# Expert weights on ScalarE, sums of gathered experts in pairs, and selection waits at their use

## The chip, the cores and the metric

The kernel is one program on one core of a Trainium2 chip. The metric is the device time of that core in microseconds. The core's engines are TensorE (PE), VectorE (DVE), ScalarE (ACT), GpSimd (POOL) and SyncE (SP), each with its own stream of instructions in a fixed order, which wait for one another by semaphores, and 16 DMA engines shared by all queues.

## The reference

One layer of a streaming encoder on x of 1024 tokens by 1024 channels, all in float32.

- Mixer: h = adaLN(RMSNorm(x)); an input projection gives q, k, v for stick-breaking attention (8 heads of 64, strictly causal), q, k, v for sliding-window attention (8 query heads, 2 key heads, chunks of 64, two chunks seen, ALiBi and sinks), and two gates. Each branch is projected to 1024 channels, they are merged with sigmoid gates, and x gets gate1 times the output projection.
- Channel part (PEER): h2 = adaLN(RMSNorm(x)). For each token and each of 8 heads: 2 x 128 sub-key scores, top 16 of each half, 256 candidate sums, top 16 of these. That gives 128 experts per token, of 16384. Each expert is one row u and one row v of 1024 floats:

```
act = gelu(h2 . u[e])            exact gelu
w   = softmax(best scores)[e] * act
y   = sum over the token's 128 experts of w * v[e]
x   = x + gate2 * y, then a final RMSNorm
```

## The kernel before

**Gathers.** The table `uv` holds each expert's u and v side by side, 8 KB a row. Tokens are worked in 8 blocks of 128. A block has 128 tiles, and a tile is 128 gathered rows: of 32 tokens, four experts each (partition 32 q + t). GpSimd issues one indirect DMA per tile (L524) into a ring of RING = 10 slots (`ring`), after it has waited for `vs_done` of the group of tiles to which the tile 10 before belongs (L522). The i-th tile serves token group c = i % 4 (32 tokens each).

**What a tile goes through.** VectorE multiplies the u half with the tokens' replicated h2 row (`h2rep[:, c]`) and sums it into one column of `dots` (L1371). For each group of STEP = 4 tiles ScalarE makes gelu of four columns (L1086, `gl`). VectorE multiplies with the gates (L1383, `wv`), and multiplies a stack of four 32x32 unit matrices (`istack`) by these per-partition weights (L1386, `dg`, 128x32 per tile). TensorE multiplies `dg` with the v half, in two halves of 512 columns, into the PSUM banks VACC and VACC+1, one 32-row band per token group (L874); that sum over a block's 128 tiles is y. Its last matmul counts `vs_done`, which frees the ring slots.

**At the end of a block** VectorE takes y out of PSUM (L1397) once all sums of the block are done, and the first sums of the next block wait for that (`fin_y`). Before it, the next block's h2 rows are replicated: for each token group c, four times TensorE (L860) and ScalarE (L1078, `rep_ev`) pass a 256-column piece over one PSUM bank (MISC), each step waiting for the one before; ScalarE's copy for c waits until the old block's last dot product with `h2rep[:, c]` is done.

**Selection** of the experts (`keys`, VectorE) runs in 32 chunks (2 heads of a block each) some 64 tiles ahead: max, max_index, match_replace and so on, each of which waits for the one before through `link` (class Chain: the instruction counts a semaphore and the engine waits for it at once). Between the steps the stream yields, so dot products come in. `gates` makes the softmax's Exp and copies the published indices and gates (L1056, L1062, L1064).

**The mixer** runs in three groups of 2, 3 and 3 blocks (SIZE). The first (g=0) comes before all gathers; the other two run beside the gathers of earlier blocks. Its stages in order: H (norm), V, QK and SB (four head pairs of stick-breaking attention, `pair`), SWP and SW (windowed attention), MG (merge), OUT, PREP (the scores for the selection). Weights are loaded by SP's queue. In SB, ScalarE does Abs, Exp, Ln and again Exp per step (L1017, L1022, L1027, L1035) between TensorE and VectorE.

**The order of the work** is written by `interleave`: every stream yields places, counted in tiles, and the engine's instructions are emitted by rising place. `Plan` gives the mixer's items their places: an item of so many microseconds takes us / rate places, with RATES = (1.9, 3.1, 2.0) for the three groups; g=1 begins at place 0, g=2 at place 235. The tile streams have the places i (dot of tile i), 4(n+1) - 0.9 (gelu of group n), 4(n+1) - 0.4 (weights), 4(n+1) - 0.2 (sums); the replicates for block b have 128 b - 3.6 + c on TensorE and 128 b - 3.5 + c on ScalarE. Since each engine runs its stream in order, an instruction that waits holds back everything of that engine that has a later place.

**ScalarE's function tables** are loaded by an instruction of their own, which `Tables.use` (L98) puts ahead of a function if another table is active at that point of the order: GELU (also used for Tanh), EXP_LN, SQRT. Copy, Abs and Square need no change of table.

Of the kernel before, what the change touches and what calls it, by code (L numbers as in the profile page):

```python
# [14 lines left out]
P = 128  # L15
# [24 lines left out]
RATES = (1.9, 3.1, 2.0)  # L40
# [4 lines left out]
STEP = 4  # L45
# [32 lines left out]
class Chain:  # L78
# [101 lines left out]
def build(nc, x, c8, w_ada, b_ada, g1, g2, gf, w_v, w_qk, w_sw, sinks, w_mg, w_out, w_q, sk, uv, consts,  # L180
          x1_dram, h2_dram, mods_dram, k_dram, v_dram, s_dram, out):
    with ExitStack() as ctx:
# [3 lines left out]
        def sem(name):  # L186
            return ctx.enter_context(nc.semaphore(name))
# [35 lines left out]
        wv = sb("wv", [P, 8])  # L223
# [56 lines left out]
        dve_own = sem("dve_own")  # L280
# [28 lines left out]
        dots_done, gelu_done, dg_done, vs_done = sem("dots_done"), sem("gelu_done"), sem("dg_done"), sem("vs_done")  # L309
# [25 lines left out]
        with nc.Block() as block:  # L335
# [192 lines left out]
            def _(pe):  # L528
# [353 lines left out]
            def _(act):  # L882
# [218 lines left out]
            def _(dve):  # L1101
                link = Chain(dve, dve_own)

# [180 lines left out]
                def keys():  # L1284
                    def top16(values, indices, scores):
                        apart(dve, dve_steps)
                        link(dve.max(values[:, 0:8], scores))
                        yield
                        apart(dve, dve_steps)
                        link(dve.max_index(indices[:, 0:8], values[:, 0:8], scores))  # L1290
                        yield
                        apart(dve, dve_steps)
                        link(dve.match_replace(scores, values[:, 0:8], scores, LOWEST))
                        yield
                        apart(dve, dve_steps)
                        link(dve.max(values[:, 8:16], scores))
# [173 lines left out]
```

## Time and profile before

| | |
|---|---|
| median of 3 runs | 3722.71 us (3718.5 to 3725.89) |
| profiled execution, own time | 3718.71 us |
| its span, first to last instruction | 3716.9 us |
| mean granted TensorE clock | 0.765 |
| busy: PE / DVE / ACT / POOL | 2262.8 / 2161.4 / 685.8 / 1137.3 us |
| moved by DMA | 1276.05 MB, mean 343 GB/s |
| first gather issued, last gather issued | 446.4 and 3689.2 us |

Times in the rows below are microseconds from the start of the span unless they are marked ns. A row of a window gives each engine's busy time with its number of instructions, then the granted TensorE clock, the mean busy share of the 16 DMA engines and the GB/s. A row of a group gives the count, total busy time and mean ns of one, and the idle time of the engine just before them with what ended it. "L874" is line 874 of the kernel. The profiled execution's time is 1.8 us over its span.

### The profile page before, as it was taken

What the parts mean: (1) busy time and instruction counts of PE and PEld (TensorE: products, weight loads), DVE (VectorE), ACT (ScalarE), POOL (GpSimd) and SP (SyncE); (2) the same over time, 40 slices, a digit from 0 to 9 for tenths busy, and PEclk for the clock granted to TensorE, in tenths of its full rate; (3) what the DMA queues carried; (4) which work ended last, traced back from release to release, by engine and by line L of the source; (5) the groups of instructions that cost most, each with busy time, mean ns of one, the idle gap of its engine ahead of it and who ended that gap; (6) DMA issues with size and microseconds to landing.
All of it is one profiled execution on the core that took longest, in us unless ns stands there. A gap on an engine that the chain in (4) does not pass through costs nothing. (4 is left out here: it accounts for less than half of the span.)

```text
span 3716.9 us, 34683 instructions
## 1 busy us (share of the span) xinstructions
PE 2262.8 (61%) x11240; PEld 998.4 (27%) x11240; DVE 2161.4 (58%) x5280; ACT 685.8 (18%) x1587; POOL 1137.3 (31%) x1033
## 2 busy tenths in 40 slices
PE   4678766875987837677776877683433343334333
PEld 2466623333433412232233432341000000000000
DVE  1011444666556465777767766566576767776754
ACT  1210113522102111544422002110100010001000
POOL 0000112322223233333333423334344434443443
PEclk8889868987998967888887989786565556556656
DMA  6414557887799998999988998999899989998998
GB/s 261 171 72 164 194 214 300 340 330 287 315 370 372 362 403 324 352 369 374 355 354 355 422 421 339 374 420 419 351 396 421 417 338 421 421 420 335 421 421 338
DMA packets 196254, 1276.05 MB, mean 343 GB/s; under 512 B 21260, under 2 KB 38700, under 8 KB 54632
## 3 DMA queue, kind: packets, MB, share of 16 engines
q0 software_dynamic: 147616, 1074.03, 71.3%
q1 hardware_dynamic: 48456, 199.80, 13.8%
q8 instruction: 89, 1.46, 0.2%
q14 instruction: 93, 0.76, 0.1%
HBM read 1249.35 MB, written 24.40 MB: 343 GB/s over the span
## 5 line engine op out<-in xcount | busy, mean ns | idle before, releaser
L524 POOL DMA_INDIRECT arena<-in_uv,idx_r x1024 | 1134.2, 1108 | 2552.5 <-PE pb L874 1873.9
L1371 DVE CUSTOM_DVE_ANT_0 arena<-arena 128x1024 f32<-128x1024 f32 x1024 | 1250.9, 1224 | 440.3 <-DMA arena<-in_uv,idx_r 419.6
L874 PE MATMUL pb<-arena,dg 128*32 128x512 f32 x4096 | 757.7, 878 | 946.1 <-DVE dg L1386 939.0
L874 PEld LDWEIGHTS pb<-arena,dg 128*32 128x32 f32 x4096 | 136.0, 140 | 1466.0 <-DVE dg L1386 1159.7
L1086 ACT ACTIVATE gl<-dots 128x4 f32<-128x4 f32 x256 | 52.4, 205 | 1347.0 <-DVE dots L1371 1346.1
L659 PE MATMUL pb<-arena 128*128 128x384 f32 (+1 forms) x768 | 253.4, 488 | 60.2 <-DMA arena<-in_sk 32.9
L98 ACT ACT_TABLE_LOAD x178 | 228.4, 1283 | 241.2 <-DVE dots L1371 196.4
L594 PE MATMUL pb<-arena 128*128 128x384 f32 (+1 forms) x768 | 238.0, 465 | 27.5 <-DMA arena<-in_w_mg 27.5
L1383 DVE TENSOR_TENSOR wv<-gl,gate_r 128x4 f32<-128x4 f32 x256 | 41.2, 161 | 308.8 <-ACT gl L1086 275.9
L659 PEld LDWEIGHTS pb<-arena 128*128 128x128 f32 x768 | 154.3, 206 | 151.1 <-issue 78.0
L594 PEld LDWEIGHTS pb<-arena 128*128 128x128 f32 x768 | 147.8, 195 | 115.9 <-issue 49.5
L860 PE MATMUL pb<-arena,ident 128*32 128x256 f32 x1024 | 109.4, 509 | 71.7 <-ACT arena L1078 62.2
L623 PE MATMUL pb<-arena 128*128 128x512 f32 x256 | 123.2, 635 | 48.4 <-DMA arena<-in_w_out 47.5
L679 PE MATMUL pb<-arena 128*128 128x384 f32 (+1 forms) x384 | 128.0, 492 | 38.4 <-DMA arena<-in_w_qk 38.4
L1255 DVE SCALAR_TENSOR_TENSOR arena<-pb,arena 128x384 f32<-128x384 f32 (+2 forms) x120 | 51.7, 472 | 145.5 <-ACT arena L1027 124.4
L597 PE MATMUL pb<-arena 128*128 128x384 f32 (+1 forms) x384 | 116.8, 455 | 0.0
L679 PEld LDWEIGHTS pb<-arena 128*128 128x128 f32 x384 | 78.0, 208 | 90.7 <-DMA arena<-in_w_qk 41.4
L707 PE MATMUL pb<-arena,tri 128*128 128x384 f32 (+2 forms) x240 | 95.0, 489 | 8.7 <-DVE arena L1255 8.1
L1215 DVE SCALAR_TENSOR_TENSOR arena<-arena,pb 128x384 f32<-128x384 f32 (+1 forms) x48 | 24.4, 508 | 123.0 <-PE pb L597 119.1
L597 PEld LDWEIGHTS pb<-arena 128*128 128x128 f32 x384 | 72.6, 191 | 45.0 <-issue 9.8
L1371 DVE DVE_READ_ACCUMULATOR2_ANT dots<- 128x1 f32 x1024 | 84.1, 82 | 0.0
L721 PE MATMUL pb<-arena 128*64 128x384 f32 (+2 forms) x240 | 62.9, 467 | 31.9 <-ACT arena L1035 28.9
(153 smaller groups left out, 2211.9 us busy)
## 6 DMA issues: line engine op xcount, KB each, us to landing
arena<-in_w_mg SPq DMA_DIRECT2D x24, 1536.0 KB
arena<-in_w_ada SPq DMA_DIRECT2D x12, 2048.0 KB, 17.3
arena<-in_w_q SPq DMA_DIRECT2D x24, 1024.0 KB
arena<-in_uv,idx_r POOLq DMA_INDIRECT x1024
arena<-in_w_qk SPq DMA_DIRECT2D x12, 1024.0 KB, 13.0
arena<-in_w_out SPq DMA_DIRECT2D x3, 4096.0 KB, 16.3
arena<-in_w_sw SPq DMA_DIRECT2D x3, 3072.0 KB, 13.9
arena<-in_x SPq DMA_DIRECT2D x16, 512.0 KB, 20.0
```

What stands on the lines that cost most here:

```text
L98: self.act.add_instruction(mybir.InstLoadActFuncSet(name=self.nc.get_next_instruction_name(), act_func_set_id=table, engine=mybir.EngineTy ...
L524: pool.indirect_dma_start(ring[:, i % RING, :], None, uv, bass.IndirectOffsetOnAxis(ap=idx_r[:, b % 2, 4 * n + c:4 * n + c + 1], axis=0)). ...
L594: m = pe.matmul(bank, wmg[ft % 2][:, q * KT + k, :], hT[:, k, 0:T], start=(k == 0), stop=(k == KT - 1))
L597: m = pe.matmul(bank, wmg[ft % 2][:, 16 + (q - 2) * 4 + k, :], y[:, k, 0:T], start=(k == 0), stop=(k == 3))
L623: m = pe.matmul(pb[:, BGB + 2 * (j % 2) + i, :], merged[:, k, j * P:(j + 1) * P], wout[:, k, i * HALF:(i + 1) * HALF], start=(k == 0), sto ...
L659: m = pe.matmul(pb[:, BGB + p, 0:T], wq[h % 2][:, p, k, :], h2T[:, k, 0:T], start=(k == 0), stop=(k == KT - 1))
L679: m = pe.matmul(pb[:, BGB + i, 0:T], wqk[p % 2][:, i * KT + k, :], hT[:, k, 0:T], start=(k == 0), stop=(k == KT - 1))
L707: m = pe.matmul(pb[:, BGB + c % 4, 0:T - lo], tri[:], spl[:, c % 4, 0:T - lo], start=False, stop=True, skip_group_check=True)
L721: pe.matmul(pb[64 * e:64 * e + 64, AVB, lo:T], vp[:, s, 64 * e:64 * e + 64], zl[:, c % 4, 0:T - lo], start=(i == 0), stop=(s == 0), skip_g ...
L860: x_ = pe.matmul(pb[32 * q:32 * q + 32, MISC, 256:512], selector(c), h2cur[:, 256 * i:256 * i + 256], start=True, stop=True)
L874: m = pe.matmul(pb[32 * c:32 * c + 32, VACC + i, :], dg[:, STEP * n // 4 % 2, c, :], ring[:, (STEP * g + c - first) % RING, D + i * HALF:D ...
L1371: dve.tensor_tensor_reduce(u, h2rep[:, c, :], u, 1.0, 0.0, ALU.mult, ALU.add, dots[:, i % 8:i % 8 + 1]).then_inc(dots_done, 1)
```

## The change

- `STEP` becomes 2: gelu, weights, sums and the release of ring slots go by two tiles. RATES become (1.9, 2.9, 1.9).
- VectorE's stream `weights` and the buffer `wv` go. ScalarE makes `ig` = istack times the gate (one Copy with a per-partition scale for each tile, place 2(g+1) - 2.5), then the gelu (place 2(g+1) + 0.0), and after waiting for both of them and for a free `dg`, `dg` = ig times gelu, again one Copy for each tile.
- TensorE's sums move from place 4(n+1) - 0.2 to 2(n+1) + 0.8.
- The dot products get a wait for the gelu eight tiles back, since nothing else on VectorE now orders the two.
- In `keys`, `link` becomes `step.mark` at the instruction and `step.hold` ahead of the next one, after the yield; with a semaphore of its own (`dve_keys`). `tk_used` is now counted by the last step on the scores.

The diff, cut to its core:

```diff
@@ -37,12 +37,12 @@
 GROUP = [g for g in range(GROUPS) for _ in range(SIZE[g])]
 GMAX = max(SIZE)
 TMAX = GMAX * P
-RATES = (1.9, 3.1, 2.0)
+RATES = (1.9, 2.9, 1.9)
 
 RING = 10
 TILES = 128
 QUADS = TILES // 4
-STEP = 4
+STEP = 2
 STEPS = TILES // STEP
 CHUNKS = 4
 PER_CHUNK = 32
@@ -80,8 +80,14 @@
         self.eng, self.sem, self.n = eng, sem, 0
 
     def __call__(self, ins):
+        self.mark(ins)
+        self.hold()
+
+    def mark(self, ins):
         ins.then_inc(self.sem, 1)
         self.n += 1
+
+    def hold(self):
         self.eng.wait_ge(self.sem, self.n)
 
 
@@ -865,7 +871,7 @@
                         for n in range(STEPS):
                             g = STEPS * b + n
                             first = STEP * n % 4
-                            yield TILES * b + STEP * (n + 1) - 0.2
+                            yield TILES * b + STEP * (n + 1) + 0.8
                             pe.wait_ge(dg_done, g + 1)
                             if n == 0 and b:
                                 pe.wait_ge(fin_y, b)
@@ -1078,12 +1084,27 @@
                                 act.activation(h2rep[:, c, 256 * i:256 * i + 256], pb[:, MISC, 256:512], ACT.Copy).then_inc(rep_ev, 1)
 
                 def gelus():
-                    for g in range(NB * STEPS):
-                        yield STEP * (g + 1) - 0.9
-                        act.wait_ge(dots_done, STEP * (g + 1))
-                        table.use(GELU)
-                        a = STEP * g % 8
-                        act.activation(gl[:, a:a + STEP], dots[:, a:a + STEP], ACT.Gelu).then_inc(gelu_done, 1)
+                    for b in range(NB):
+                        for n in range(STEPS):
+                            g = STEPS * b + n
+                            a, first, half = STEP * g % 8, STEP * n % 4, STEP * n // 4 % 2
+                            yield STEP * (g + 1) - 2.5
+                            if STEP * n % PER_CHUNK == 0:
+                                act.wait_ge(pub_g, CHUNKS * b + STEP * n // PER_CHUNK + 1)
+                            for c in range(STEP):
+                                op = act.activation(ig[:, half, first + c], istack[:], ACT.Copy, scale=gate_r[:, b % 2, STEP * n + c:STEP * n + c + 1])
+                            op.then_inc(ig_done, 1)
+                            yield STEP * (g + 1) + 0.0
+                            act.wait_ge(dots_done, STEP * (g + 1))
+                            table.use(GELU)
+                            act.activation(gl[:, a:a + STEP], dots[:, a:a + STEP], ACT.Gelu).then_inc(gelu_done, 1)
+                            act.wait_ge(gelu_done, g + 1)
+                            act.wait_ge(ig_done, g + 1)
+                            if STEP * g >= 8:
+                                act.wait_ge(vs_done, g + 1 - 8 // STEP)
+                            for c in range(STEP):
+                                op = act.activation(dg[:, half, first + c], ig[:, half, first + c], ACT.Copy, scale=gl[:, a + c:a + c + 1])
+                            op.then_inc(dg_done, 1)
 
                 def final():
                     for b in range(NB):
@@ -1284,17 +1306,21 @@
                 def keys():
                     def top16(values, indices, scores):
                         apart(dve, dve_steps)
-                        link(dve.max(values[:, 0:8], scores))
+                        step.mark(dve.max(values[:, 0:8], scores))
                         yield
+                        step.hold()
                         apart(dve, dve_steps)
-                        link(dve.max_index(indices[:, 0:8], values[:, 0:8], scores))
+                        step.mark(dve.max_index(indices[:, 0:8], values[:, 0:8], scores))
                         yield
+                        step.hold()
                         apart(dve, dve_steps)
...
                                 op = yield from top16(vals[q][:, h, :], kidx[q][:, h, :], tk[:, n % 2, 256 * h + 128 * q:256 * h + 128 * q + 128])
+                                if h + q == 2:
+                                    op.then_inc(tk_used, 1)
+                                else:
+                                    step.mark(op)
                                 yield
-                        op.then_inc(tk_used, 1)
                         dve.wait_ge(tk_used, n + 1)
-                        link(dve.tensor_tensor(cand, vals[0][:].unsqueeze(3).to_broadcast([P, 2, TOPK, TOPK]),
-                                               vals[1][:].unsqueeze(2).to_broadcast([P, 2, TOPK, TOPK]), ALU.add))
+                        step.hold()
+                        step.mark(dve.tensor_tensor(cand, vals[0][:].unsqueeze(3).to_broadcast([P, 2, TOPK, TOPK]),
+                                                    vals[1][:].unsqueeze(2).to_broadcast([P, 2, TOPK, TOPK]), ALU.add))
                         yield
+                        step.hold()
                         for h in range(2):
-                            op = yield from top16(best[:, h, :], bidx[:, h, :], cand[:, h].rearrange("p i j -> p (i j)"))
...
@@ -1367,24 +1405,10 @@
                                 dve.wait_ge(gathered[i % RING], 16 * (i // RING + 1))
                                 if n == 0:
                                     dve.wait_ge(rep_ev, 16 * b + 4 * c + 4)
+                                if i >= 8 and i % STEP == 0:
+                                    dve.wait_ge(gelu_done, (i - 8) // STEP + 1)
                                 u = ring[:, i % RING, 0:D]
                                 dve.tensor_tensor_reduce(u, h2rep[:, c, :], u, 1.0, 0.0, ALU.mult, ALU.add, dots[:, i % 8:i % 8 + 1]).then_inc(dots_done, 1)
-
-                def weights():
-                    for b in range(NB):
-                        for n in range(STEPS):
-                            g = STEPS * b + n
-                            yield TILES * b + STEP * (n + 1) - 0.4
-                            a, first = STEP * g % 8, STEP * n % 4
-                            w = wv[:, a:a + STEP]
-                            dve.wait_ge(gelu_done, g + 1)
-                            if STEP * n % PER_CHUNK == 0:
-                                dve.wait_ge(pub_g, CHUNKS * b + STEP * n // PER_CHUNK + 1)
-                            link(dve.tensor_tensor(w, gl[:, a:a + STEP], gate_r[:, b % 2, STEP * n:STEP * (n + 1)], ALU.mult))
-                            if STEP * g >= 8:
-                                dve.wait_ge(vs_done, g + 1 - 8 // STEP)
-                            dve.tensor_tensor(dg[:, STEP * n // 4 % 2, first:first + STEP], istack[:].unsqueeze(1).to_broadcast([P, STEP, 32]),
-                                              w.unsqueeze(2).to_broadcast([P, STEP, 32]), ALU.mult).then_inc(dg_done, 1)
 
                 def final():
                     for b in range(NB):
```

## Rows read from the trace of the kernel before

**Rows 1.** The page's 40 slices, DMA.
```profile
DMA  6414557887799998999988998999899989998998
```

**Rows 2.** Windows, a late stretch: busy per engine, clock, DMA share, GB/s.
```profile
2800.00:2900.00 100.00, 35.54 (x192) 6.47 (x192) 70.79 (x180) 5.17 (x15) 38.59 (x38) 0.55 1.01 421
```

**Rows 3.** Timeline of the tail: start, duration, engine, line, idle before.
```profile
3701.22 1.23 DVE L1371 CUSTOM_DVE_ANT_0 arena<-arena 128x1024 f32<-128x1024 f32 x1 [1.22 <-DMA arena<-in_uv,idx_r]
...
3702.49 0.20 ACT L1086 ACTIVATE gl<-dots 128x4 f32<-128x4 f32 x1 [9.67 <-DVE dots L1371]
...
3702.73 0.16 DVE L1383 TENSOR_TENSOR wv<-gl,gate_r 128x4 f32<-128x4 f32 x1 [0.27 <-ACT gl L1086]
...
3706.98 1.23 DVE L1397 TENSOR_TENSOR arena<-pb,arena 128x1024 f32<-128x1024 f32 x1 [3.77 <-PE pb L874]
```

**Rows 4.** Windows of the mixer stretches.
```profile
500.00:600.00 100.00, 63.39 (x250) 26.91 (x254) 51.45 (x126) 18.80 (x43) 18.42 (x16) 0.70 0.52 204
...
500.00:1400.00 900.00, 649.97 (x3044) 312.45 (x3048) 525.48 (x1287) 210.26 (x474) 255.81 (x232) 0.85 0.84 331
...
1400.00:2600.00 1200.00, 850.42 (x4164) 363.79 (x4160) 805.38 (x1970) 312.72 (x674) 422.77 (x375) 0.84 0.93 375
```

**Rows 5.** Windows around block boundaries.
```profile
974.00:1034.00 60.00, 53.69 (x323) 25.22 (x323) 24.87 (x59) 15.99 (x35) 13.38 (x13) 1.00 0.71 279
...
3026.00:3041.00 15.00, 9.90 (x68) 2.00 (x64) 3.87 (x9) 4.06 (x9) 0.94 (x1) 0.57 0.05 18
...
3351.00:3411.00 60.00, 29.75 (x228) 6.49 (x232) 32.45 (x84) 14.01 (x31) 18.40 (x17) 0.59 0.73 287
```

**Rows 6.** Timeline of the boundary near 3020 us.
```profile
3013.36 0.38 ACT L1078 ACTIVATE arena<-pb 128x256 f32<-128x256 f32 x1 [0.76 <-PE pb L860]
...
3027.81 0.38 ACT L1078 ACTIVATE arena<-pb 128x256 f32<-128x256 f32 x1 [1.20 <-PE pb L860]
...
3035.65 3.47 PE L874 MATMUL pb<-arena,dg 128*32 128x512 f32 x16
...
3039.97 0.94 POOL L524 DMA_INDIRECT arena<-in_uv,idx_r  x1 [22.75 <-PE pb L874]
```

**Rows 7.** Groups of VectorE, each shape by itself.
```profile
L1386 DVE TENSOR_TENSOR dg<-istack,wv 128x128 f32<-128x128 f32 x256 | 74.7, 292 | 9.0 <-DVE wv L1383 0.3
...
L1383 DVE TENSOR_TENSOR wv<-gl,gate_r 128x4 f32<-128x4 f32 x256 | 41.2, 161 | 308.8 <-ACT gl L1086 275.9 <-issue 27.8 <-DVE kidx L1290 0.9
```

**Rows 8.** Waits in one attention pair (g=2), 1599.2 to 1666.9 us.
```profile
ACT L98 <- DVE dots L1371: 14.0, 5, 4.0
...
ACT arena L1017 <- PE pb L692: 8.7, 3, 5.0
...
DVE wv L1383 <- ACT gl L1086: 5.0, 4, 1.6
...
ACT arena L1035 <- PE pb L712: 4.3, 3, 1.9
```

**Rows 9.** Groups of ScalarE, each shape by itself.
```profile
L98 ACT ACT_TABLE_LOAD x178 | 228.4, 1283 | 241.2 <-DVE dots L1371 196.4 <-PE pb L594 16.1 <-DVE stats L1182 7.2
...
L1022 ACT ACTIVATE arena<-arena 128x256 f32<-128x256 f32 x24 | 8.8, 431 | 0.0
...
L937 ACT ACTIVATE arena<-arena,stats 128x192 f32<-128x192 f32 x56 | 24.6, 441 | 0.1
...
L1056 ACT ACTIVATE best<-best 128x32 f32<-128x32 f32 x32 | 7.3, 229 | 3.8 <-DVE best L1340 3.5
```

**Rows 10.** Windows of that pair: all engines, then the table loads alone.
```profile
1599.20:1666.90 67.70, 48.83 (x214) 18.24 (x212) 56.52 (x143) 39.18 (x76) 23.61 (x20) 0.87 0.92 354
...
1599.20:1666.90 67.70, 15.40 (x12) 0.87 0.92 354
```

**Rows 11.** Timeline of ScalarE in that pair.
```profile
1614.47 1.28 ACT L98 ACT_TABLE_LOAD   x1
...
1615.77 0.20 ACT L1086 ACTIVATE gl<-dots 128x4 f32<-128x4 f32 x1
```

More of the change, by code:

```diff
@@ L222, in build @@
         gl = sb("gl", [P, 8])
-        wv = sb("wv", [P, 8])
+        ig = sb("ig", [P, 2, 4, 32])
         dg = sb("dg", [P, 2, 4, 32])
@@ L1102, in _ @@
                 link = Chain(dve, dve_own)
+                step = Chain(dve, dve_keys)
                 def start():
@@ L1319, in one @@
                             if q == 0:
-                                link(dve.tensor_scalar(part_u[:], bidx[:], 4, None, ALU.logical_shift_right))
+                                step.mark(dve.tensor_scalar(part_u[:], bidx[:], 4, None, ALU.logical_shift_right))
                             else:
-                                link(dve.tensor_scalar(part_u[:], bidx[:], TOPK - 1, None, ALU.bitwise_and))
+                                step.mark(dve.tensor_scalar(part_u[:], bidx[:], TOPK - 1, None, ALU.bitwise_and))
@@ L1323, in one @@
                             yield
-                            link(dve.tensor_copy(fl[q][:], part_u[:]))
+                            step.hold()
+                            step.mark(dve.tensor_copy(fl[q][:], part_u[:]))
                             yield
-                            link(dve.tensor_tensor(wide, fl[q][:].rearrange("p b k -> p (b k)").unsqueeze(2).to_broadcast([P, 2 * TOPK, TOPK]),
-                                                   iota16[:].unsqueeze(1).to_broadcast([P, 2 * TOPK, TOPK]), ALU.is_equal))
+                            step.hold()
@@ L1328, in one @@
+                            step.mark(dve.tensor_tensor(wide, fl[q][:].rearrange("p b k -> p (b k)").unsqueeze(2).to_broadcast([P, 2 * TOPK, TOPK]),
+                                                        iota16[:].unsqueeze(1).to_broadcast([P, 2 * TOPK, TOPK]), ALU.is_equal))
                             yield
-                            link(dve.tensor_copy(fl[q][:], kidx[q][:]))
-                            link(dve.tensor_tensor(cand, cand, fl[q][:].unsqueeze(2).to_broadcast([P, 2, TOPK, TOPK]), ALU.mult))
+                            step.hold()
@@ L1331, in one @@
+                            step.mark(dve.tensor_copy(fl[q][:], kidx[q][:]))
+                            step.hold()
+                            step.mark(dve.tensor_tensor(cand, cand, fl[q][:].unsqueeze(2).to_broadcast([P, 2, TOPK, TOPK]), ALU.mult))
                             yield
-                            link(dve.tensor_reduce(res[q][:].rearrange("p b k -> p (b k)"), wide, AX, ALU.add))
+                            step.hold()
+                            step.mark(dve.tensor_reduce(res[q][:].rearrange("p b k -> p (b k)"), wide, AX, ALU.add))
@@ L1333, in one @@
                             yield
+                            step.hold()
                         if b >= 2:
                             dve.wait_ge(pub_mm, n - 2 * CHUNKS + 1)
-                        link(dve.scalar_tensor_tensor(out=picks[:, b % 2, m, 0, :], in0=res[0][:].rearrange("p b k -> p (b k)"), scalar=float(NKEYS),
-                                                      in1=res[1][:].rearrange("p b k -> p (b k)"), op0=ALU.mult, op1=ALU.add))
+                        step.mark(dve.scalar_tensor_tensor(out=picks[:, b % 2, m, 0, :], in0=res[0][:].rearrange("p b k -> p (b k)"), scalar=float(NKEYS),
+                                                           in1=res[1][:].rearrange("p b k -> p (b k)"), op0=ALU.mult, op1=ALU.add))
@@ L1338, in one @@
                         yield
-                        link(dve.tensor_copy(norm[:], best[:, :, 0]))
+                        step.mark(dve.tensor_copy(norm[:], best[:, :, 0]))
+                        step.hold()
                         dve.tensor_tensor(best[:], best[:], norm[:].unsqueeze(2).to_broadcast([P, 2, TOPK]), ALU.subtract).then_inc(picked, 1)
@@ L1407, in final @@
                         dve.scalar_tensor_tensor(out=yfin, in0=yfin, scalar=stats[:, 50:51], in1=final_row, op0=ALU.mult, op1=ALU.mult).then_inc(fin_done, 1)
-                interleave(start(), mods(), dot_products(), weights(), keys(), final(), *[mixer(g) for g in range(GROUPS)])
+                interleave(start(), mods(), dot_products(), keys(), final(), *[mixer(g) for g in range(GROUPS)])
 def shape_constants():
```

13 lines of the change are left out of this document (8 added, 5 removed).

## The prediction

> **What bounds the kernel now.** I read the page's forty slices first, then windows, the boundary between two blocks in order of time, the waits of one attention pair, the groups of ScalarE, and the tail. In the slices the DMA row stands at 8 or 9 from slice 10 on [rows 1]; in a late window it is at 1.01 and moves 421 GB/s while VectorE is busy 71 of 100 us and TensorE 36 [rows 2]. A gathered tile is 128 rows of 8 KB, 1.05 MB; at 421 GB/s that is 2.49 us, and a late dot product is 1.22 us of waiting for the gather and 1.23 us of work [rows 3]. So the gathers and weight loads are the bound wherever they run. What can be won is the time in which the DMA engines are idle; what can be lost is more of it.
>
> The windows say where they are idle [rows 4]. From 500 to 1400 us, in which the second group (g=1) of the mixer runs, the share is 0.84, that is 900 x 0.16 = 144 us idle; from 1400 to 2600, where the third group (g=2) runs, 0.93, 84 us. Later only block boundaries are left. Seven windows of 60 us around the boundaries have shares from 0.70 to 0.80, together 1.80 windows or 108 us missing (the first and the last of the seven are shown, 0.71 and 0.73 [rows 5]); four of them, 60 us by the same sum, lie inside the two stretches above. Outside boundaries there are 144 + 84 - 60 = 168 us, of which 48 are the start (500 to 600 us, share 0.52). The budget for a gain is thus 108 us at boundaries and 120 in mixer stages.
>
> **A boundary, step by step.** Between 3026 and 3041 us the DMA share is 0.05: 14 us idle [rows 5]. GpSimd issues nothing for 22.75 us, until the sums of the old block's last four tiles are done [rows 6]. These sums stand in TensorE's order behind all sixteen replicate steps (copy and wait, 0.38 + 0.76 = 1.14 us, to 0.38 + 1.20 = 1.58 us each); their gelu stands in ScalarE's order behind twelve of these and two table loads; VectorE's L1397 stands behind the sums.
>
> **The change part by part.**
>
> Sums in pairs. The slots of gathered tiles come free after 2 tiles and 8 matmuls, not 4 and 16; TensorE takes 3.5 us for the sixteen [rows 6], so 1.8 us for eight. "One tile later" moves the place in TensorE's order from -0.2 to +0.8. The mean hold of a slot in places is nearly the same (a tile of four waits 0 to 3 places less 0.2, after it one of two waits 0 or 1 place plus 0.8: 1.3 both times), the longest falls from 2.8 to 1.8. In the late stretch this gives nothing: DMA is full there [rows 2].
> At a boundary I go through the new order with these durations. The next-to-last pair is now summed after the third set of replicate steps, ahead of the fourth: two slots come free near 3032 where the row has 3040. The last pair needs its gelu and copies after the fourth set, and its sums come after these: near 3041.5, against 3039. The gap of 14 us becomes one of about 7 and one of 4. Gain 3 us, x 7 = 21. Bounds: it may lose 3 us each (the last pair, and L1397 with it, later by 2 to 4 us) or gain 8: +21 to -56.
>
> ScalarE makes the weights. VectorE loses 256 x (161 + 292) ns = 116 us of work and its waits on gelu, 276 us [rows 7]. In the late stretch it has slack: nothing. In the mixer stages its softplus and copies no longer stand behind gelu; in one attention pair this wait is 5.0 of 67.7 us [rows 8]. ScalarE gains 1024 copies of istack with the gate as scale, 1024 with gelu as scale, and 256 more gelus of 0.20 us. A 128x32 operation with immediates takes 229 ns and one of 256 elements 431, by which 192 elements would take 373; with a per-partition bias they take 441, so such an operand costs about 70 ns [rows 9]. Bounds for a copy 0.21 to 0.30 us, taken 0.25: 2048 x 0.25 = 512 us of ScalarE over the span, 0.5 us per tile, beside 0.1 us for the gelu and, before the second copies, a wait for its own gelu of at most 0.27 us, which is what VectorE idles there [rows 3]. Against 2.49 us per tile that is hidden in the late stretch. The istack copies are placed 2.5 tiles before the gelu and are off the path from dot to sums; that path has 0.2 + 0.2 + 0.5 where it had 0.2 + 0.7 us: equal.
> By the Trainium skill, "ScalarE: Activation LUTs" (What ACT_TABLE_LOAD costs), an ACTIVATE takes 186 ns + 0.833 ns per element, plus 93 ns for a pointer operand: an estimate of 306 ns per copy, or 213 where two overlap. No row shows such a copy; by the upper figure the copies would be 627 us.
>
> Table loads. They follow from the static order: gelu needs one table, Exp and Ln another, each switch is a load of 1283 ns, and the trace has 178 [rows 9]. I put the places of all users of a table on one line and counted the switches: 177 for before (the first load is the 178th); for after (pairs, place +0.0, the new rates) 222. Of the 45 more, 15 are in the attention of g=1 and 34 to 36 in that of g=2; elsewhere the changes cancel. 45 x 1.283 = 58 us of ScalarE.
> In the attention pair from 1599.2 to 1666.9 us ScalarE is busy 39.2 of 67.7 us, 15.4 of it in 12 loads [rows 10], and waits 14.0 us for dots and 8.7 + 4.3 for TensorE [rows 8]. After: 39 + 9 loads (11.5) + 25 tiles x 0.5 (12.5) + 6 gelus (1.3) + own waits (2) = 66 of then about 70 us (25.0 tiles at rate 1.9, where 23.8 stood). ScalarE comes close to being the bound of this stage. But most of the 14.0 us of waiting for dots comes from the gelu's place at -0.9, ahead of the dot's end; at +0.0 it is due after it. The addition that this wait does not absorb is 27 - 14 = 13 us per pair in g=2, half of that in g=1: bounds 0 to 80 us. I take 5 us per pair in g=2 and 2.5 in g=1, 30 us, nearer the low end since both engines have slack in the QK part of each pair.
> The same page and section puts a table switch at 2.66 us with its drain. The trace disagrees: a load begun at 1614.47 us is followed by its gelu at 1615.77 [rows 11], 1.30 us. By the page the 45 loads would cost 120 us of ScalarE, and the attention of g=2 would surely lengthen.
>
> Rates 3.1 to 2.9 and 2.0 to 1.9. The plan divides each item by the rate, so g=1 ends at place 218 (was 206) and g=2 at 595 (was 578). 12 and 17 more gathers stand beside mixer work: 29 x 2.49 = 72 us if the mixer alone set the pace of all of it, nothing where DMA is already full. Of the 120 us of idle I take a quarter, 30 us, for this, for the shorter longest hold and for VectorE's freed waits together. Bounds: 0 to -75.
>
> Selection. About 45 chained steps in each of 32 chunks now wait just before the next step, behind a dot product that has come between. VectorE spends under 0.2 us each with work; it gains only where VectorE is late, which the late stretch excludes: 0, bounds 0 to -10. The one added wait, for a gelu eight tiles back, is met some five tiles before it is asked: 0; queued behind it would be the dots and, through them, everything.
>
> Tail. From the last dot's end, 3702.5, to L1397, 3707.0, are 4.5 us [rows 3]; with 8 matmuls and the copies near 3: -1.5.
>
> Sum: -21 + 30 - 30 - 1.5 = -22.5, against the profiled execution's 3718.7 us (3716.9 of span and 1.8 around it), which lies 4.0 under the median of the three runs, 3722.7. From the median: 3700 us.
>
> **The rivals.**
> 1. ScalarE becomes the bound of the attention stages. 66 of 70 us leaves no room for the 13 us of waits on TensorE in the pair, which are in one chain with it. Price 13 x 4 + 6.5 x 4 = 78 us on top of the stage; the other gains, 52 us, are partly eaten by it, half say: +52, but the slower stage also lets DMA finish its weight loads, -20: about 3755 us. It decides once a pair of g=2 takes over 80 us. For: ScalarE is 0.58 busy before any addition, 0.94 after. Against: 14 us of waiting for dots go.
> 2. The mixer fills with gathers better than taken: the idle share in g=1 falls from 0.16 to 0.10 (-54), boundaries lose 6 us less each (-42), attention costs 15: 3722.7 - 81 = 3642 us. For: slots are what GpSimd waits for [rows 6, 8], and they come in pairs. Against: much of that wait is only the queue of a full DMA.
> 3. All cancels, since DMA is at 0.93 where most of the change acts and the late stretch is untouched: 3722 us.
>
> **Numbers.** A measurement of this kernel tells 0.2%, 7.4 us, from no change. Forecast (3680 to 3714) 0.40; rival 2 and what lies between it and the forecast 0.22; rival 3 (3715 to 3730) 0.11; rival 1 and milder forms of it 0.27. The likeliest case's own range is 3670 to 3714; over all cases, with 2 in 10 left out at the two ends, 3640 to 3755. Faster 0.62, same 0.11, slower 0.27.
>
> **What would show it.** Right: 222 to 224 table loads; 2.49 us per tile after 2700 us; boundary windows with shares up by 0.05 and two separate gaps; DMA's share from 500 to 1400 us at 0.87; attention pairs of g=2 of 70 to 75 us with ScalarE over 0.85 busy. Wrong: boundary windows with lower shares, pairs over 80 us, copies over 0.30 us each, or a late stretch slower than 2.49 us per tile.

## The result, and the profile after

The changed kernel takes 3739.33 us in the median (3732.58 to 3741.44, 4 runs) against 3720.61 us of the kernel before on the same chip: a ratio of 1.0046, with a 95% interval from 1.0027 to 1.0066. It is slower by 0.3 to 0.7%, where 0.6% faster was forecast. The profiled execution has a span of 3738.5 us. One execution of a run below (e1, 3994.95 us) fell into the chip's slower state, and it is left out of that run's median and ratio.

The groups of the kernel after (line, engine, operation, count, busy us, mean ns, idle before and its releaser), beside [rows 7, 9]:

```profile
L880 PE MATMUL pb<-arena,dg 128*32 128x512 f32 x4096 | 1209.3, 731 | 595.7 <-ACT dg L1106 594.0 <-issue 1.5
...
L104 ACT ACT_TABLE_LOAD x223 | 286.1, 1283 | 90.0 <-DVE dots L1411 35.3 <-PE pb L600 11.3 <-DVE stats L1428 11.0
...
L1106 ACT ACTIVATE dg<-ig,gl 128x32 f32<-128x32 f32 x1024 | 273.0, 314 | 16.9 <-ACT gl L1100 0.2
...
L1095 ACT ACTIVATE ig<-istack,gate_r 128x32 f32<-128x32 f32 x1024 | 265.2, 306 | 0.0
```

and the same group of TensorE before the change, which the forecast did not show:

```profile
L874 PE MATMUL pb<-arena,dg 128*32 128x512 f32 x4096 | 757.7, 878 | 946.1 <-DVE dg L1386 939.0 <-issue 6.6
```

The sums have the same 4096 matmul records (a float32 matmul is two of them), but TensorE is busy with them for 1209.3 us where it was 757.7. The reason is in the timelines. A group of four tiles before (first fence) and a group of two after (second fence), both at the 2.4 GHz clock:

```profile
1518.45 1.92 PE L874 MATMUL pb<-arena,dg 128*32 128x512 f32 x16 [2.29 <-DVE dg L1386]
```

```profile
1655.40 1.91 PE L880 MATMUL pb<-arena,dg 128*32 128x512 f32 x8 [2.50 <-ACT dg L1106]
```

Sixteen records on four bands of 32 rows take 1.92 us, eight on two bands 1.91 us. The bands run side by side, and what a group costs is the work of one band. Halving the group halves the work and leaves the time, so TensorE pays 1.9 us for two tiles. Where the granted clock is lower it is the same: in the late stretch, sixteen took 3.22 us before (at 2865.50) and eight took 3.28 us after (at 2869.22), which is why the totals are above 1.9 us times the number of groups.

The windows of the kernel after, to be held against [rows 4], then the attention pair of g=2 that answers to [rows 10] (all engines, then the table loads alone):

```profile
500.00:1400.00 900.00, 729.32 (x2948) 317.86 (x2950) 465.18 (x1105) 331.22 (x968) 236.02 (x216) 0.90 0.81 307
1400.00:2600.00 1200.00, 965.83 (x4188) 374.10 (x4186) 757.00 (x1804) 554.86 (x1570) 434.65 (x382) 0.92 0.95 381
2800.00:2900.00 100.00, 55.48 (x192) 9.81 (x190) 66.52 (x162) 26.18 (x105) 43.33 (x40) 0.76 1.01 421
```

```profile
1648.50:1722.30 73.80, 58.03 (x262) 20.85 (x262) 53.89 (x133) 68.30 (x151) 25.49 (x24) 0.98 0.97 389
```

```profile
1648.50:1722.30 73.80, 29.51 (x23) 0.98 0.97 389
```

In the stretch from 500 to 1400 us TensorE is busy 729 us where it was 650, and the DMA share falls from 0.84 to 0.81. By the starts of the first and last matmuls of each stage, the q and k projections of the attention of g=1 (572 to 741 us before) run from 576 to 774, the last matmul of its attention steps starts at 820 instead of 778, MG's last 63 us later, and the last of PREP at 1396 instead of 1311. Twelve more gathers stand beside it by then, so the dot of tile 288 comes 50 us late. In g=2 the share is 0.95 against 0.93 and 21 us come back; tile 656 is 29 us late. The late stretch runs at 421 GB/s in both, and a block wins some 2 us there: tile 704 is 27.9 us late, and tile 960, two blocks on, 23.6.

The attention pair came out nearly as worked out: 73.8 us for 25 tiles, ScalarE busy 68.3 (0.93), 23 table loads where 21 were added up. It isn't where the sign was lost.

### The profile page after: what moved, and what is told of

Read it like the earlier page. It is cut to its first block and busy times, and to the rows that moved or that the text cites. A ratio compares the mean times of both kernels' runs of the same rounds, so it can differ in the third digit from the quotient of the medians.

```text
span 3738.5 us, 36601 instructions
## 1 busy us (share of the span) xinstructions
PE 2671.1 (71%) x11240; PEld 1053.8 (28%) x11240; DVE 2024.8 (54%) x4768; ACT 1274.7 (34%) x3936; POOL 1150.8 (31%) x1033
## 5 line engine op out<-in xcount | busy, mean ns | idle before, releaser
L530 POOL DMA_INDIRECT arena<-in_uv,idx_r x1024 | 1147.8, 1121 | 2557.3 <-PE pb L880 1911.8
L880 PE MATMUL pb<-arena,dg 128*32 128x512 f32 x4096 | 1209.3, 731 | 595.7 <-ACT dg L1106 594.0
L880 PEld LDWEIGHTS pb<-arena,dg 128*32 128x32 f32 x4096 | 220.6, 123 | 1440.0 <-ACT dg L1106 925.0
L1100 ACT ACTIVATE gl<-dots 128x2 f32<-128x2 f32 x512 | 103.0, 201 | 1065.7 <-DVE dots L1411 1057.6
L1106 ACT ACTIVATE dg<-ig,gl 128x32 f32<-128x32 f32 x1024 | 273.0, 314 | 16.9 <-ACT gl L1100 0.2
L1095 ACT ACTIVATE ig<-istack,gate_r 128x32 f32<-128x32 f32 x1024 | 265.2, 306 | 0.0
L665 PEld LDWEIGHTS pb<-arena 128*128 128x128 f32 x768 | 149.3, 201 | 152.1 <-issue 84.9
L600 PEld LDWEIGHTS pb<-arena 128*128 128x128 f32 x768 | 145.5, 195 | 123.6 <-issue 62.5
L1309 DVE MAX8 vals<-arena 128x8 f32<-128x128 f32 x128 | 37.0, 289 | 134.9 <-DMA arena<-s_scratch 134.9
L1084 ACT ACTIVATE arena<-pb 128x256 f32<-128x256 f32 x128 | 49.0, 383 | 168.1 <-PE pb L866 162.3
L685 PEld LDWEIGHTS pb<-arena 128*128 128x128 f32 x384 | 76.8, 206 | 100.0 <-DMA arena<-in_w_qk 47.4
L993 ACT ACTIVATE arena<-pb 128x384 f32<-128x384 f32 (+1 forms) x48 | 21.7, 454 | 241.6 <-PE pb L665 231.2
```

The costliest lines, as they stand in the source:

```text
L530: pool.indirect_dma_start(ring[:, i % RING, :], None, uv, bass.IndirectOffsetOnAxis(ap=idx_r[:, b % 2, 4 * n + c:4 * n + c + 1], axis=0)). ...
L600: m = pe.matmul(bank, wmg[ft % 2][:, q * KT + k, :], hT[:, k, 0:T], start=(k == 0), stop=(k == KT - 1))
L665: m = pe.matmul(pb[:, BGB + p, 0:T], wq[h % 2][:, p, k, :], h2T[:, k, 0:T], start=(k == 0), stop=(k == KT - 1))
L685: m = pe.matmul(pb[:, BGB + i, 0:T], wqk[p % 2][:, i * KT + k, :], hT[:, k, 0:T], start=(k == 0), stop=(k == KT - 1))
L880: m = pe.matmul(pb[32 * c:32 * c + 32, VACC + i, :], dg[:, STEP * n // 4 % 2, c, :], ring[:, (STEP * g + c - first) % RING, D + i * HALF:D ...
L1095: op = act.activation(ig[:, half, first + c], istack[:], ACT.Copy, scale=gate_r[:, b % 2, STEP * n + c:STEP * n + c + 1])
```

## The experiments

Ratios are to the kernel before on the same chip, with their 95% intervals. The kernel before took 3711.8 to 3721.9 us in the sets of runs, so runs of different sets are held against each other by their ratios. Four runs came first, to take the change apart.

**The changed kernel with the old rates (e1).**

```diff
-RATES = (1.9, 2.9, 1.9)
+RATES = (1.9, 3.1, 2.0)
```

> The changed kernel with the old rates (3.1, 2.0); everything else of the change stays. ScalarE theory (45 more table loads and 2048 copies of 0.31 us lengthen the attention stages, the rates only hide or show it): the mixer is as late as with the new rates or later, 3740 us or more, about 3745. Rates theory (the stretched plan itself costs, since in MERGE and PREP the gathers set the pace): the loss is mostly gone, 3715 to 3727 us.

3762.73 us, 1.0112 (1.0076 to 1.0148). The rest of the change costs 1.1% by itself, and the new rates hide more than half of it.

**The kernel before with the new rates (e2).**

```diff
-RATES = (1.9, 3.1, 2.0)
+RATES = (1.9, 2.9, 1.9)
```

> The kernel before with the new rates (2.9, 1.9) and nothing else. ScalarE theory: no loss from the rates alone, 3705 to 3725 us, the attention of g=1 as long as before to within 10 us. Rates theory: most of the 17 us of loss is here, 3735 us or more.

3664.27 us, 0.9849 (0.9819 to 0.9879). The rates alone make the kernel 1.5% faster, more than either theory said: 56 us, beyond even the 30 us that the forecast gave to rates, slots and VectorE together. By the dots' times the whole gain is made in g=1: tile 192 comes 56 us earlier than before, tile 656 55. The windows, against [rows 4]:

```profile
500.00:1400.00 900.00, 664.14 (x3148) 315.86 (x3149) 561.05 (x1363) 212.47 (x481) 278.25 (x247) 0.86 0.87 347
1400.00:2600.00 1200.00, 828.76 (x4150) 356.67 (x4148) 809.44 (x1996) 306.12 (x668) 428.31 (x382) 0.84 0.94 382
```

**The changed kernel in fours (e3).**

```diff
-STEP = 2
+STEP = 4
```

> The changed kernel with STEP = 4: ScalarE still makes the weights (2048 copies), but gelu, sums and slots go by four tiles, so the table loads fall back to about 174. ScalarE theory, if the table loads are what costs: attention of g=1 20 us shorter than in the changed kernel, 3715 to 3728 us. If the copies cost: no shorter, 3740 or more. Against both, a theory that the pairs bring a gain through earlier slots says 3745 us or more, since that gain goes and each slot is then held one place longer.

3687.98 us, 0.9912 (0.9883 to 0.9941), with 176 table loads. The q and k projections of g=1 end at 740 us instead of 774. All of the loss and more hangs on the pairs; whether on their table loads or on TensorE this run can't say.

**The kernel before in pairs (e4).**

```diff
-STEP = 4
+STEP = 2
```

> The kernel before with STEP = 2: VectorE makes the weights for two tiles at a time, old places, old rates. ScalarE theory, table loads: some 45 or more loads come in, the attention of g=1 lengthens by 15 us or more, 3735 us or more. If it is the copies on ScalarE that cost: the slots' gain stands alone, 3695 to 3715 us.

3843.00 us, 1.0333 (1.0306 to 1.0361), with 231 loads. The pairs are the costly part, 122 us on VectorE's weights. I had looked at table loads so far; TensorE's 1252 us of sums in this run led to the timelines above, and to two theories: TensorE's time, or the 53 more loads.

**Order of the bands (e7), on the kernel before.**

```diff
-                            for i in range(2):
-                                for c in range(first, first + STEP):
+                            for c0, i in ((0, 0), (0, 1), (2, 0), (2, 1)):
+                                for c in range(c0, c0 + 2):
```

> The kernel before, with the sixteen matmuls of a group of four tiles issued in another order: both halves of row bands 0 and 1, then both halves of 2 and 3, so that two bands stand side by side in place of four. Same count of matmuls, same groups, same table loads, old rates. TensorE theory (what the pairs cost is that two of TensorE's four 32-column groups stand idle, so 8 matmuls take the 1.92 us of 16): a group takes 3.8 us at 2.4 GHz instead of 1.92, and the kernel takes 3790 us or more, most of the 122 us that VectorE's pairs alone cost. Table-load theory: the order changes nothing that matters, 3715 to 3735 us.

3709.56 us, 0.9999 (0.9989 to 1.0010). Both numbers of the TensorE theory fail here, but the run didn't make the state that it was meant to: a group still takes 1.94 us at 2.4 GHz. In the records, the first matmuls of bands 2 and 3 begin 0.03 us after those of 0 and 1. TensorE fills all four bands in this order too. So it needs a wait to keep bands apart.

**Halves of the bands in turn, by a wait (e10), on the kernel before.**

```diff
-                            for i in range(2):
-                                for c in range(first, first + STEP):
...
+                            for c0 in (0, 2):
+                                for i in range(2):
+                                    for c in (c0, c0 + 1):
...
+                                if c0 == 0:
+                                    m.then_inc(vs_half, 1)
+                                    pe.wait_ge(vs_half, g + 1)
```

> The kernel before, where TensorE waits after the eight matmuls of row bands 0 and 1 until they are done, and then does bands 2 and 3. So a group of four tiles takes 2 x 1.92 us, as it does in pairs, with groups, table loads and rates as before. TensorE theory: 3780 us or more, most of the 122 us that the pairs alone cost on VectorE's weights. Table-load theory: 3710 to 3735 us.

3886.87 us, 1.0435 (1.0410 to 1.0459), the largest loss of all. The busy time of the sums, and in the timeline a group at the full clock:

```profile
L875 PE MATMUL pb<-arena,dg 128*32 128x512 f32 x4096 | 1248.4, 740 | 728.4 <-DVE dg L1390 696.7 <-issue 14.2 <-PE pb L875 0.2
```

```profile
1603.19 3.89 PE L875 MATMUL pb<-arena,dg 128*32 128x512 f32 x16 [2.29 <-DVE dg L1390]
```

3.89 us for four tiles, 178 table loads, gelu and weights as before: TensorE's time is enough for a loss of this size. It even exceeds e4, whose slots at least come free in twos; TensorE's wait for itself is also part of it, and so are the slots of a group's first two tiles, which are held through both halves. So the run shows that the time costs, and not how much it costs in the change.

**Pairs with sums in fours (e11), on the kernel before.** Gelu and VectorE's weights go by two tiles, sums and slots by four (the waits that count `vs_done` are changed to match, not shown).

```diff
-STEP = 4
+STEP = 2
...
-                        for n in range(STEPS):
+                        for n in range(QUADS):
...
-                            yield TILES * b + STEP * (n + 1) - 0.2
-                            pe.wait_ge(dg_done, g + 1)
+                            yield TILES * b + 4 * (n + 1) - 0.2
+                            pe.wait_ge(dg_done, 4 // STEP * (g + 1))
```

> The kernel before, with gelu and VectorE's weights in pairs (some 231 table loads), but the sums and the release of slots in fours, so that a group of sums takes 1.92 us again; old rates. TensorE theory: 3710 to 3745 us, the 122 us of the full pairs mostly gone. Table-load theory: 3790 us or more.

3794.10 us, 1.0192 (1.0174 to 1.0210): the table-load theory's number, and only 1.4% come back from e4 with TensorE's sums at 763.5 us. With e10 this makes 4.35% and 1.9% for the two parts where both together cost 3.3%: the slots that come free in twos repay some, and the wait on TensorE in e10 costs some. So on VectorE's weights TensorE's time is not the whole loss. But these 72 us for 53 loads are 1.4 us each, three times what a load costs in e5 and e6 below (0.42 us), so the loads alone don't explain them either. VectorE's wait for gelu, 276 us in [rows 7], is longer; that this is the rest of it is argued and not tested:

```profile
DVE wv L1382 <- ACT gl L1085: 368.7, 210, 19.8
```

**The changed kernel with sums in fours (e12).** The same edit of the sums, on the changed kernel.

```diff
-                            yield TILES * b + STEP * (n + 1) + 0.8
-                            pe.wait_ge(dg_done, g + 1)
+                            yield TILES * b + 4 * (n + 1) + 0.8
+                            pe.wait_ge(dg_done, 4 // STEP * (g + 1))
```

> The changed kernel with its gelu and weights in pairs on ScalarE, but sums and slots in fours. TensorE theory: most of the 50 us that lie between the changed kernel (1.0046 of before) and the same with all in fours (0.9912) come back, 3675 to 3700 us. Table-load theory: nothing comes back, 3730 us or more.

3699.94 us, 0.9938 (0.9916 to 0.9961): 1.1% come back, at the edge of what the TensorE theory said, while the table-load theory's 3730 is far. This kernel has all of the change (223 table loads among it) but the sums and slots in pairs. Its group of sums, and its windows:

```profile
L879 PE MATMUL pb<-arena,dg 128*32 128x512 f32 x4096 | 739.2, 859 | 869.9 <-ACT dg L1105 855.1 <-issue 14.7
```

```profile
500.00:1400.00 900.00, 658.36 (x3064) 313.25 (x3064) 503.25 (x1190) 352.38 (x1032) 260.94 (x236) 0.84 0.84 334
1400.00:2600.00 1200.00, 842.23 (x4184) 362.33 (x4184) 766.28 (x1811) 548.47 (x1565) 424.13 (x382) 0.85 0.94 382
```

With e3 at 0.9912, pairs of gelu and of ScalarE's weights cost 0.26%, and the intervals overlap, so that this may be nothing.

Held against e12 tile by tile, the changed kernel shows where the pairs of sums cost. Its dot of tile 64 comes 23 us after e12's, tile 128 36, tile 192 59, tile 256 63 us (1504.1 against 1441.3): all of it in g=1, whose attention, MG, OUT and PREP stand beside these tiles. From 256 to 512 nothing is added. From tile 512 on the pairs win: 63 us become 53 at tile 704 and 42 at 960, in the late stretch some 5.5 us a block. That is what the slots that come free in twos are worth. TensorE is busy 729 us between 500 and 1400 us in the one and 658 in the other. A rival would be that pairs make TensorE's stream stop twice as often for weights that are not yet there. It doesn't hold: from 500 to 1400 us its weight loads for sums wait 70.0 us for `dg` with pairs and 77.4 us with fours.

**What table loads cost (e5, e6).** Gelu becomes a Copy that needs no load, in the changed kernel (e5) and in the one before (e6).

```diff
-                            table.use(GELU)
-                            act.activation(gl[:, a:a + STEP], dots[:, a:a + STEP], ACT.Gelu).then_inc(gelu_done, 1)
+                            act.activation(gl[:, a:a + STEP], dots[:, a:a + STEP], ACT.Copy).then_inc(gelu_done, 1)
```

> The changed kernel with a Copy in the place of gelu and no table load for it, so that the expert weights are gate times dot without gelu: the loads that gelu causes are gone, the pairs stay. Table-load theory: the loss goes with them and the kernel gains beyond, 3680 us or less. TensorE theory: the sums still take 1.9 us for two tiles and set the pace of the mixer stages; what goes is the smaller part, 3705 to 3735 us.

> The kernel before with a Copy in the place of gelu and no table load for it, so that the weights are gate times dot without gelu; groups, sums and rates as before. It is the control for the same edit in the changed kernel, which took 0.9819 of before from 1.0046: 2.3% for some 186 loads. If a load costs the same in both, the 140 loads less here are worth 1.7%, 3650 to 3665 us. If loads cost mostly where ScalarE is full of pairs and copies, 3680 to 3705 us.

Both leave gelu out. e5: 3646.06 us, 0.9819 (0.9802 to 0.9835) with 37 loads. e6: 3664.54 us, 0.9843 (0.9821 to 0.9866) with 39. I had expected e5 to stay over 3705 by the TensorE theory. It counted only the 45 new loads and forgot that e5 drops the 140 old ones as well. Per load, e6 gives 1.57% x 3720 / 139 = 0.42 us of the end time, e5 2.27% x 3720 / 186 = 0.45: a third of the 1.283 us that ScalarE spends, in both kernels. If a new load costs what the average one does, the 45 new ones are worth 20 us.

**The selection's waits (e8, e14).** Every step of the selection waits for the one before at its use, on the kernel before: e8 with the new rates, e14 with the old ones. The edit, at one of its places:

```diff
-                        link(dve.max(values[:, 0:8], scores))
+                        step.mark(dve.max(values[:, 0:8], scores))
                         yield
+                        step.hold()
```

> The kernel before with the new rates and the selection's waits at their use, nothing else; to be held against 3664 us with the new rates alone. My forecast's view, that these waits are hidden: 3657 to 3671 us. The view that VectorE is late in the mixer stages: 3640 to 3656 us.

> The kernel before with the selection's waits at their use and nothing else, old rates. My forecast took nothing for it. New rates with and without it stand at 0.9784 and 0.9849 of before: if its gain doesn't hang on the rates, 3693 to 3702 us; if VectorE gave a gain only where the rates had made room, 3712 us or more.

e8: 3633.92 us, 0.9784 (0.9768 to 0.9800), against 0.9849 for the rates alone. e14: 3698.94 us, 0.9950 (0.9932 to 0.9969). The edit I had priced at nothing gains 0.5% at the old rates, and the difference at the new ones is 0.65%. In e14 the gain is made before the late stretch: the dot of tile 704 comes 23.0 us earlier than before, the last one 25.7. Where a dot product's rows have landed, it starts behind a selection step with no gap. Such places with the wait at once (e2, first fence) and at its use (e8):

```profile
2128.55 0.29 DVE L1296 MAX8 vals<-arena 128x8 f32<-128x128 f32 x1
2128.88 1.23 DVE L1371 CUSTOM_DVE_ANT_0 arena<-arena 128x1024 f32<-128x1024 f32 x1
```

```profile
2113.15 0.29 DVE L1306 MAX8 vals<-arena 128x8 f32<-128x128 f32 x1
2113.36 1.21 DVE L1394 CUSTOM_DVE_ANT_0 arena<-arena 128x1024 f32<-128x1024 f32 x1
```

The dot begins 0.04 us after the end of the step in the one and 0.08 us before it in the other. Over the whole traces, 283 dots of the kernel before start 0.03 to 0.04 us after the end of a selection step, and 329 of e14 0.08 to 0.09 us before it. Some 300 times 0.11 us are 33 us of VectorE's time, of which those in the mixer stages count.

**ScalarE's weights at the old places, in fours (e9).** All of the change but pairs and later places (the copies of istack move with the gelu, from 2.5 tiles before their group's end to 3.4).

```diff
-STEP = 2
+STEP = 4
...
-                            yield TILES * b + STEP * (n + 1) + 0.8
+                            yield TILES * b + STEP * (n + 1) - 0.2
...
-                            yield STEP * (g + 1) + 0.0
+                            yield STEP * (g + 1) - 0.9
```

> The changed kernel with STEP = 4 and the old places (istack copies -3.4, gelu -0.9, sums -0.2), ScalarE still makes the weights; to be held against 3688 us with quads at the new places. If the later place costs slots (each held one place longer): 3665 to 3678 us. If it is the copies on ScalarE that cost the 24 us against the new rates alone: 3684 us or more, and more than that if the later place spared waits.

3655.18 us, 0.9854 (0.9836 to 0.9873). Against e3 (0.9912, from another set of runs) the later places cost 0.6%. Against e8, run beside it and differing by ScalarE's weights, those cost 0.7%, 21 us (3655.18 less 3633.92). Of my two readings both hold in part.

**Still lower rates (e13), on e8.**

```diff
-RATES = (1.9, 2.9, 1.9)
+RATES = (1.9, 2.8, 1.8)
```

> The kernel before with the selection's waits at their use and still lower rates (2.8, 1.8); to be held against 0.9784 of before at the rates 2.9, 1.9. If the mixer stages still set the pace with gathers waiting beside them, more places for the mixer gain again, 0.970 to 0.976 of before. If DMA is full there by now, or the last group's scores come late for the selection, 0.977 to 0.985.

3661.38 us, 0.9837 (0.9821 to 0.9854): worse than e8's 0.9784. The gain from the rates turns near the values of the change. Which of the named limits ends it was not looked into.

## Why the prediction was wrong, step by step

Along the runs, the change adds up like this, in ratios to the kernel before:

| | ratio | step |
|---|---|---|
| new rates (e2) | 0.9849 | -1.5% |
| and the selection's waits (e8) | 0.9784 | -0.65% |
| and ScalarE's weights, in fours (e9) | 0.9854 | +0.7% |
| and the later places (e3) | 0.9912 | +0.6% |
| and gelu and weights in pairs (e12) | 0.9938 | +0.3%, not clear of noise |
| and sums and slots in pairs (the change) | 1.0046 | +1.1% |

The steps hang on the order in which they are taken: the new rates bring 1.5% on the kernel before, and 0.66% where the rest of the change is there already (e1, 1.0112, against 1.0046).

**Sums in pairs: the step that failed.** I wrote that TensorE takes 3.5 us for sixteen, "so 1.8 us for eight". It takes the same time for eight, 1.91 us against 1.92 at the full clock. I had the row with x16 and four bands before me [rows 6] and divided by the count of matmuls. The code says what had to be divided: each tile of a group writes a 32-row band of its own (L874). This added 452 us of TensorE work (1209.3 - 757.7), where I had added none, and TensorE was the busiest engine of the stretch from 500 to 1400 us, 650 of 900 us. The cost fell in the mixer of g=1, 63 us by tile 256 against e12. The step's other half, that slots come free earlier, is real but small: some 5.5 us a block in the late stretch. e10 shows that doubling TensorE's time is enough for a loss, e12 what undoing the pairs of sums gives back in this kernel, 1.1% or 40 us.

Without this step the kernel stands at 3699.94 us (e12) where 3700 was forecast. That is luck: the rates brought 26 us more than was taken for them, and the selection some 20 us where nothing was taken. Against that, the later places cost 22 us that are not in the sum, and the 21 us that were to be won at the boundaries don't come in e12, which loses 3.3 us a block to the kernel before from tile 704 to 960.

The Trainium skill, "TensorEngine Tiling (Array Packing)", section Tiling Modes, says that 128x32 makes four tiles of the array which work in parallel. The trace agrees (16 records in the time of 8). By that rule a group that fills two of the four takes twice the time per tile, and TensorE's part of the sum would not have stood at nothing.

**Rates: right sign, too small.** Taken within -30 us, alone worth -56 (e2). The bound of 72 us, 29 gathers beside mixer work, was the nearer end, but they don't all count: the gain is there at tile 192, beside g=1, and the 17 gathers more beside g=2 added nothing.

**Selection: priced at nothing.** It is worth -19 us (e14). I argued from the late stretch, where VectorE has slack, and bounded the rest at 10 us; of the 25.7 us that e14's profile gains, 23.0 are made before the late stretch, where VectorE's time counts.

**ScalarE's weights.** Copies of 0.31 us, not 0.25, just over my upper bound of 0.30. Two in a row overlap (0.53 us for both in the timelines), so that they are busy for 538 us where 512 were taken. The estimate from the Trainium skill's "ScalarE: Activation LUTs" (What ACT_TABLE_LOAD costs) of 306 ns agrees with the rows, 306 and 314 ns. The 223 table loads are as counted (222); 0.3% for pairs of gelu and 0.7% for the copies make 36 us by this table, where 30 were charged. The 0.7% is what is left after VectorE's freed work, which the forecast had counted with the rates. Rival 1 had the right sign, and 3755 us is not far off, but by luck: its engine was ScalarE, and the pairs over 80 us that were to decide it didn't come (73.8 us for the one that was read).

**Later places.** Costed at nothing by an equal mean hold, measured at +0.6% between two sets of runs. In the late stretch, over the two blocks from tile 704 to 960, e3 loses 9.8 us on the kernel before and e9, with the old places, 0.7: some 4.5 us a block. In the kernel after VectorE waits 143.0 us for the sums at L1421 (before: 45.1 us of idle at L1397, all eight blocks together) and 134.9 us for the selection's scores (before: 49.6). The later places make less than half of the first increase and nothing of the second: e9, with the old places, has 102.0 us at L1421, where e3 has 144.7 and e8, without ScalarE's weights, 34.9, and its wait for scores is 111.6 us against 101.4 in e3. By which wait the later places cost their time is open.

**Boundaries.** The gap has the two parts that were worked out. The kernel after, around the boundary near 3060 us:

```profile
3050.00:3054.00 4.00, 1.18 (x40) 0.61 (x40) 0.00 (x0) 3.02 (x9) 0.00 (x0) 0.87 0.99 410
3054.00:3058.00 4.00, 2.52 (x20) 0.40 (x16) 0.00 (x0) 1.15 (x3) 0.00 (x0) 0.50 0.34 137
3058.00:3062.00 4.00, 3.61 (x24) 1.07 (x24) 0.00 (x0) 0.67 (x2) 0.00 (x0) 0.78 0.00 2
3062.00:3066.00 4.00, 1.92 (x24) 0.47 (x24) 0.00 (x0) 1.69 (x7) 1.87 (x2) 1.00 0.60 184
3066.00:3070.00 4.00, 3.33 (x8) 0.53 (x8) 0.39 (x1) 0.61 (x3) 0.00 (x0) 0.57 0.83 332
3070.00:3074.00 4.00, 0.00 (x0) 0.00 (x0) 3.82 (x8) 0.70 (x4) 2.22 (x2) 0.93 0.51 170
```

Almost nothing moves from 3056 to 3062, then two tiles, then a second dip. A block of the late stretch wins some 2 us by the dots' times; 3 were forecast. By the runs that is two effects of some 5 us against each other, slots in twos and later places.

**Tail.** From the last dot's end to L1421 are 2.8 us; near 3 were forecast.

**The signs.** Of the five that were to show the forecast right, three came: 223 loads, 421 GB/s late, and a pair of 73.8 us. The boundary windows came half: the three late ones are at 0.84, 0.79 and 0.80 (0.70, 0.75 and 0.73 before), the four beside the mixer at 0.72, 0.74, 0.64 and 0.80 (0.71, 0.76, 0.80 and 0.75). The DMA share from 500 to 1400 us, 0.81 where 0.87 was to stand, showed the loss. (Rival 2 names [rows 8] beside [rows 6] for GpSimd's wait for slots; only [rows 6] shows it.)

The version that beats both is e8: the new rates and the selection's waits at their use, with VectorE's weights and groups of four, at 3633.92 us, 2.2% under the kernel before.

## What to carry to other kernels

Before a group of matmuls is halved, look at which bands of the array it fills: here the time went by the work of one band, not by the count, and half a group cost the whole. Price an edit in the stage where its engine is in the chain, not in the stage where it has slack. And where a change bundles a retuned order with new work, ask what the order alone is worth: here it gained 1.5% by itself and hid more than half of what the rest lost.

## What the runs showed of the hardware that was not expected

TensorE started the matmuls of different bands side by side in both orders that were run (e7: 1.94 us, bands 2 and 3 begun 0.03 us after 0 and 1, though both halves of bands 0 and 1 stood ahead of them).

With the same 192 records spread over more of the time, TensorE has more of the full clock: in the late stretch, 2800 to 2900 us, the granted clock is 0.76 after and 0.55 before [rows 2], that is more of it at 2.4 and less at 1.2 GHz, with TensorE busy 55 against 36 of 100 us.

A table load of 1.283 us, in a stream shared with latency-bound work, cost 0.42 to 0.45 us of the end time on average (e5, e6).
